# Triangular inversion of a chunked delta rule with its two 64-blocks laid over each other

## What is computed

```python
def gated_delta_chunked(q, k, v, g, beta, state0):
    ...
    decay = jnp.exp(jnp.where(incl, Gcum[..., :, None] - Gcum[..., None, :], -jnp.inf))
    kb = kc * bc[..., None]
    A = jnp.where(strict, jnp.einsum('bhnid,bhnjd->bhnij', kb, kc) * decay, 0.0)
    t_inv = lax.linalg.triangular_solve(A + eye, jnp.broadcast_to(eye, A.shape), left_side=True, lower=True, unit_diagonal=True)
    W = t_inv @ (kb * jnp.exp(Gcum)[..., None])
    U = t_inv @ (vc * bc[..., None])
    attn = jnp.einsum('bhnid,bhnjd->bhnij', qc, kc) * decay
    ...
    def step(S, xs):
        W_n, U_n, attn_n, qd_n, kt_n, gt_n = xs
        v_new = U_n - jnp.einsum('bhcd,bhde->bhce', W_n, S)
        o = jnp.einsum('bhcd,bhde->bhce', qd_n, S) + jnp.einsum('bhij,bhje->bhie', attn_n, v_new)
        S = S * gt_n[..., None, None] + jnp.einsum('bhcd,bhce->bhde', kt_n, v_new)
        return S, o
```

## Time and profile before

| | us |
|---|---|
| median of 3 runs | 1768.65 (1767.53 to 1769.34) |
| the profiled execution's own time | 1769.91 |
| its span on the core | 1768.1 |
| PE busy | 1712.0 |
| PE weight loads busy | 1535.7 |
| DVE busy | 1299.4 |
| ACT busy | 1075.2 |
| POOL busy | 161.9 |

### The profile page before, as it was taken

The page is one execution under the profiler, slowest core; times in us unless marked ns, Lnnn a source line. Parts: engine busy times, 40 slices in busy tenths (PEclk is TensorE's granted clock), DMA queues, the critical chain, the costliest instruction groups (busy, mean ns, idle before and its releaser), DMA issues.

```text
span 1768.1 us, 34099 instructions
## 1 busy us (share of the span) xinstructions
PE 1712.0 (97%) x11488; PEld 1535.7 (87%) x11488; DVE 1299.4 (73%) x2604; ACT 1075.2 (61%) x2222; POOL 161.9 (9%) x136
## 2 busy tenths in 40 slices
PE   7999998999999999999999999999899999999998
PEld 1877788989999977888899999999799899999997
DVE  3787667767989799667766666666776668878887
ACT  2545466645665699666555555555558666666666
POOL 0000004411638200000000000000010000010000
PEclk9899999999999999999999999999999999999999
DMA  8524441225455411555555555555354544555553
GB/s 301 185 99 143 153 158 62 82 71 190 158 178 188 157 37 38 180 193 196 190 190 184 185 189 185 184 189 190 119 205 143 172 137 134 178 184 185 189 181 129
DMA packets 77271, 283.30 MB, mean 160 GB/s; under 512 B 8576, under 2 KB 8576, under 8 KB 76928
## 3 DMA queue, kind: packets, MB, share of 16 engines
q1 hardware_dynamic: 77184, 282.16, 47.5%
HBM read 281.08 MB, written 1.05 MB: 160 GB/s over the span
## 4 chain that ended last, share of the span: by engine, by line
PE 80%; DVE 11%; ACT 5%; issue 1%; DMA 1%; POOL 1%; PEld 0%; PEldq 0%; SPq 0%; ACTq 0%; POOLq 0%; DVEq 0%
PE banks L901 20%; PE banks L889 17%; PE banks L980 9%; PE banks L491 8%; PE banks L1136 7%; PE banks L1160 3%; PE banks L831 2%; DVE split L2396 2%; DVE arena L2392 2%; PE banks L459 1%; DMA arena<-wstream 1%; PE banks L994 1%; PE banks L680 1%; PE banks L1096 1%; PE banks L665 1%
## 5 line engine op out<-in xcount | busy, mean ns | idle before, releaser
L1501 ACT ACTIVATE split<-arena 128x512 fp32r<-128x512 f32 x492 | 308.9, 629 | 135.0 <-PE banks L889 76.8
L889 PEld LDWEIGHTS banks<-split 128*128 128x128 f32 x2880 | 355.4, 192 | 10.5 <-DVE split L2322 3.1
L901 PE MATMUL banks<-split 128*128 128x512 f32 x1536 | 361.9, 390 | 1.0 <-issue 1.0
L889 PE MATMUL banks<-split 128*128 128x256 f32 x2880 | 358.7, 283 | 3.1 <-DVE split L2322 2.3
L2414 DVE TENSOR_TENSOR split<-arena,split 128x512 fp32r<-128x512 f32 x396 | 270.5, 690 | 105.3 <-ACT split L1501 99.5
L901 PEld LDWEIGHTS banks<-split 128*128 128x128 f32 x1536 | 283.8, 188 | 57.3 <-issue 1.4
L1479 ACT ACTIVATE split<-arena 128x512 fp32r<-128x512 f32 x312 | 194.5, 627 | 115.4 <-PE banks L1136 52.9
L980 PE MATMUL banks<-split 128*128 128x256 f32 x1728 | 218.1, 288 | 4.3 <-DVE split L2492 3.9
L980 PEld LDWEIGHTS banks<-split 128*128 128x128 f32 x1728 | 213.2, 195 | 7.2 <-issue 6.0
L2469 DVE TENSOR_TENSOR split<-arena,split 128x512 fp32r<-128x512 f32 x180 | 123.8, 698 | 67.5 <-ACT split L1479 66.0
L491 PEld LDWEIGHTS banks<-split 128*128 128x128 f32 (+1 forms) x936 | 134.3, 195 | 28.1 <-issue 14.1
(11 more groups left out here) (414 smaller groups left out, 2359.1 us busy)
## 6 DMA issues: line engine op xcount, KB each, us to landing
arena<-wstream SPq DMA_DIRECT2D x525, 512.0 KB, 3.3
arena<-x_t SPq DMA_DIRECT2D x1, 2048.0 KB, 13.0
arena<-matsa SPq DMA_DIRECT2D x1, 1234.0 KB, 6.5
out_t<-arena SPq DMA_DIRECT2D x4, 256.0 KB, 2.0
arena<-mats SPq DMA_DIRECT2D x1, 576.0 KB, 8.3
arena<-crow SPq DMA_DIRECT2D x1, 512.0 KB, 7.3
arena<-rows SPq DMA_DIRECT2D x1, 512.0 KB, 4.0
arena<-mats SPq DMA_DIRECT2D x1, 449.0 KB, 3.7
```

What stands on the lines that cost most here:

```text
L889: mm = pe.matmul(ps[:, 4 + b, 0:S], w_parts[:, c, (2 * m + half) % 4, P * k:P * k + P], h_parts[:, e, 4 * half + k, :], start=(half == 0 a ...
L901: mm = pe.matmul(ps[:, 2 * tt + half, :], g_parts[:, e, j % 2, P * tt:P * tt + P], w_parts[:, c, (2 * m + half) % 4, :], start=(first and ...
L1501: act.activation(w_parts[:, 0, (2 * m + half) % 4, :], ring[:, peer_slot(m), 512 * half:512 * half + 512], ACT.Copy).then_inc(sem["w_hi"], 1)
```

## The change

Up to level 5 nothing outside the two 64x64 diagonal blocks of each 128x128 matrix is used. The changed kernel lays these two over each other: partitions 0 to 63 hold the first block, partitions 64 to 127 the second, in the same 64 columns per head. The tiles `Z1`, `Z2` and the new `AO` (the keys laid over each other) have 4 x 64 = 256 columns instead of 512, a half of Z has 128, the packed keys have 128 per slot.

- Products: for each 64-block q one matmul with 64 rows (partitions 64q to 64q + 63), all four heads in it, into bank `2d + q`, and one transpose of 64 rows into the same bank behind it, columns 128 to 191. Order: transpose 0, transpose 1, product 0, product 1.
- One DVE eviction of both banks with a mask widened by ones (`masks`, built at the stage's start) takes products and transposes to `yp` (128 x 2 x 192). The tile `T`, ACT's copy to it and the semaphore `t_ready` are gone.
- Updates: for each q one matmul with all 128 rows and 64 output partitions, 64q to 64q + 63.
- The subtraction, `keep_half` and `pack_keys` work on 128 columns. `pack_keys` at level 1 first lays the keys over each other (two copies of 64 partitions, and a wait for them).
- Level 6 joins the two blocks: its products use the rows of one 64-block, its transposes those of the other, and its updates write the 64 partitions `rows_at(d)`. DVE evicts them in three copies for each direction, ahead of `first_inverse`, and writes the negated update to the new tile `Z` (128x512), the rest of which ACT fills from level 6's halves; the never-written quarter is set to zero at the stage's start.
- `first_inverse` takes four operations of 64 partitions x 128 columns for each direction instead of two of 128 x 256.
- `apply_inverse` writes the keys' part to bank `2d + 1`; the products of level 1 of the next step wait for `w_moved`, which ACT raises once `wt` is copied.

```diff
+        rows_at = lambda q: slice(64 * q, 64 * q + 64)
+        last_keys = lambda d: flat(pair[d]["AP"])[rows_at(1 - d), P:3 * P]
+        level_bank = lambda d, q: ps[:, 2 * d + q, :]
...
             def level_products(n, l, d):
...
                 pe.wait_ge(sem["keys_packed"], level_at(n, l, d))
-                for j in range(2):
-                    c = slice(P * j, P * j + P)
-                    mm = pe.matmul(ps[:, d, c], keys_at(d, l)[:, c], half_at(d, l, 1 - d)[:, c], start=True, stop=True)
-                mm.then_inc(sem["y_done"], 1)
                 if l == 1:
                     if n:
-                        pe.wait_ge(sem["wu_ready"], step_at(n - 1, d))
+                        pe.wait_ge(sem["w_moved"], step_at(n - 1, d))
                     else:
                         pe.wait_ge(sem["tok_ready"], 3 + d)
-                for j in range(2):
-                    mm = pe.transpose(ps[:, 2 + d, P * j:P * j + P], half_at(d, l, d)[:, P * j:P * j + P], ident)
-                mm.then_inc(sem["z_turned"], 1)
+
+                def product(q):
+                    c, r = slice(P * q, P * q + P), rows_at(q if l < 6 else 1 - d)
+                    keys, half = (keys_at(d, l)[r, :], half_at(d, l, 1 - d)[r, :]) if l < 6 else (last_keys(d)[:, c], inverse_at(d, 6)[r, c])
+                    return pe.matmul(level_bank(d, q)[:, 0:P] if l < 6 else level_bank(d, 0)[:, c], keys, half, start=True, stop=True)
+
+                def turn_half(q):
+                    c, r = slice(P * q, P * q + P), rows_at(q if l < 6 else d)
+                    half = half_at(d, l, d)[r, :] if l < 6 else inverse_at(d, 6)[r, c]
+                    return pe.transpose(level_bank(d, q)[:, P:P + 64] if l < 6 else level_bank(d, 1)[:, 64 * q:64 * q + 64], half, ident[r, r])
+
+                if l < 6:
+                    turn_half(0)
+                    turn_half(1).then_inc(sem["z_turned"], 1)
+                    product(0)
+                else:
+                    product(0)
+                    turn_half(0)
+                product(1).then_inc(sem["y_done"], 1)
+                if l == 6:
+                    turn_half(1).then_inc(sem["z_turned"], 1)
 
             def level_update(n, l, d):
                 pe.wait_ge(sem["y_out"], level_at(n, l, d))
-                pe.wait_ge(sem["t_ready"], level_at(n, l, d))
-                for j in range(2):
-                    mm = pe.matmul(ps[:, d, 256 + P * j:256 + P * j + P], pair[d]["T"][:, j, :], yp[d][:, j, :], start=True, stop=True)
+                for q in range(2):
+                    out = ps[rows_at(q), 2 * d, 256:384] if l < 6 else ps[rows_at(d), 2 * d, 256 + P * q:384 + P * q]
+                    mm = pe.matmul(out, yp[d][:, q, P:P + 64], yp[d][:, q, 0:P], start=True, stop=True)
                 mm.then_inc(sem["p_done"], 1)
...
             def pack_keys(n, l, d):
+                a, over = pair[d][f"A{n % 2}"], pair[d]["AO"].rearrange("p a (b s) -> p (a b) s", s=64)
                 if l == 1:
                     act.wait_ge(*((sem["mask_ready"], d + 1) if n == 0 else (sem["a_beta"], step_at(n - 1, d))))
-                act.activation(as_packed(keys_at(d, l), l), parts(flat(pair[d][f"A{n % 2}"]), l, d), ACT.Copy).then_inc(sem["keys_packed"], 1)
+                    for q in range(2):
+                        o = act.activation(over[rows_at(q)], a[rows_at(q), :, rows_at(q)], ACT.Copy)
+                    link(o)
+                if l < 6:
+                    o = act.activation(as_packed(keys_at(d, l), l), parts(flat(pair[d]["AO"]), l, d), ACT.Copy)
...
                     for d in range(2):
-                        if l == 6:
-                            act.wait_ge(sem["y_done"], level_at(n, l, d))
-                            for q in range(2):
-                                r = slice(64 * q, 64 * q + 64)
-                                o = act.activation(yp[d][r, :, r], bank(d, 2, P)[r, :, r], ACT.Copy)
-                            o.then_inc(sem["y_out"], 1)
-                        act.wait_ge(sem["z_turned"], level_at(n, l, d))
-                        act.activation(flat(pair[d]["T"]), ps[:, 2 + d, 0:256], ACT.Copy).then_inc(sem["t_ready"], 1)
...
+            for d in range(2):
+                dve.memset(pair[d]["Z"][rows_at(1 - d), :, rows_at(d)], 0.0)
+            dve.memset(masks[:, :, P:P + 64], 1.0)
+            link(dve.tensor_copy(masks[:, :, 0:P], blocks))
             tails = iter(range(EARLY_TAILS, 32))
...
                     for d in range(2):
+                        dve.wait_ge(sem["z_turned"], level_at(n, l, d))
+                        dve.wait_ge(sem["y_done"], level_at(n, l, d))
                         if l < 6:
-                            dve.wait_ge(sem["y_done"], level_at(n, l, d))
-                            dve.tensor_tensor(yp[d], bank(d, 2, P), bc(blocks[:, l - 1, :], 1, 2), ALU.mult).then_inc(sem["y_out"], 1)
-                        elif n < 3:
+                            o = dve.tensor_tensor(yp[d], ps[:, 2 * d:2 * d + 2, 0:P + 64], bc(masks[:, l - 1, :], 1, 2), ALU.mult)
+                        else:
+                            dve.tensor_copy(yp[d][:, :, P:P + 64], bank(2 * d + 1, 2, 64))
+                            for q in range(2):
+                                r = rows_at(q)
+                                o = dve.tensor_copy(yp[d][r, :, r], bank(2 * d, 2, P)[r, :, r])
+                        o.then_inc(sem["y_out"], 1)
+                    for d in range(2):
+                        if l == 6 and n < 3:
                             first_inverse(n + 1, d)
```

More of the change, by code:

```diff
@@ L238, in build @@
         at = buf("at", 4, 4, P)
-        PAIR = ("E", "A0", "A1", "Z0", "Z1", "Z2", "AP", "T", "KB", "VB", "KT", "S", "wt", "uu")
-        pair = [{n: buf(f"{n}{d}", 2 if n == "T" else 4, P) for n in PAIR} for d in range(2)]
-        yp = [buf(f"yp{d}", 2, P) for d in range(2)]
+        PAIR = ("E", "A0", "A1", "Z1", "Z2", "Z", "AO", "AP", "KB", "VB", "KT", "S", "wt", "uu")
+        TWO = ("Z1", "Z2", "AO")
+        pair = [{n: buf(f"{n}{d}", 2 if n in TWO else 3 if n == "AP" else 4, P) for n in PAIR} for d in range(2)]
+        yp = [buf(f"yp{d}", 2, P + 64) for d in range(2)]
+        masks = buf("masks", 5, P + 64)
         assert held["rstd"][0] == held["root"][0] + 512
@@ L655, in level_products @@
                 if l == 1:
-                    if n == 0 and d == 1:
+                    if n == 0 and d == 0:
                         pe.wait_ge(sem["proj_free"], 4 + 39)
@@ L694, in apply_inverse @@
                 for h in range(4):
-                    pe.matmul(ps[:, 2 + d, P * h:P * h + P], b["KB"][:, h, :], z[:, h, :], start=True, stop=True)
+                    pe.matmul(ps[:, 2 * d + 1, P * h:P * h + P], b["KB"][:, h, :], z[:, h, :], start=True, stop=True)
                 for h in range(4):
@@ L1422, in _ @@
                     act.wait_ge(sem["wu_done"], step_at(n, d))
-                    act.activation(pair[d]["wt"].rearrange("p a b -> p (a b)"), ps[:, 2 + d, :], ACT.Copy)
+                    act.activation(pair[d]["wt"].rearrange("p a b -> p (a b)"), ps[:, 2 * d + 1, :], ACT.Copy).then_inc(
+                        sem["w_moved"], 1)
                     act.activation(pair[d]["uu"].rearrange("p a b -> p (a b)"), ps[:, 6 + d, :], ACT.Copy).then_inc(sem["wu_ready"], 1)
@@ L2109, in first_inverse @@
                 dve.wait_ge(sem["m_turned"], step_at(n, d))
[L2110 to L2113 removed]
+                for r in (rows_at(0), rows_at(1)):
+                    for q in range(2):
+                        o = dve.tensor_tensor(half_at(d, 1, q)[r, :].rearrange("p (a b s) -> p a b s", a=4, s=2),
+                                              bc(ident[r, r].rearrange("p (b q s) -> p b q s", q=2, s=2)[:, :, q, :], 1, 4),
+                                              bank(4 + d, 4, P)[r, :, r].rearrange("p a (b q s) -> p a b q s", q=2, s=2)[:, :, :, q, :],
+                                              ALU.subtract)
                 o.then_inc(sem["z1_ready"], 1)
```

46 lines of the change are left out of this document (29 added, 17 removed).

## The result

The changed kernel is slower: 1781.78 us median of 5 runs (1772.43 to 1782.27) beside 1768.85 for the kernel before (1767.53 to 1769.83), ratio 1.0061, 95% interval 1.0039 to 1.0083. The forecast was 1764.3 with a range of 1758 to 1771. The profiled execution of after is the fastest of the five, 1772.43.

What follows compares the result with a forecast made beforehand. TensorE, busy nearly the whole span, was taken as the bound. Terms -5.0 - 1.35 - 0.5 - 1.3 + 2.95 + 0.85 = -4.35 us gave 1764.3 against the median of 1768.65, range 1758 to 1771.

Steps and rivals of the forecast that it cites:

- column groups pair: Updates on two column groups: the two matmuls pair as row groups do, taking two steps a direction; forecast 0.57.
- change of shape: Switching PE between 128-row and 64-row work costs 0.2 us a change, with two to four changes a level.
- groups A to D: Levels by kind: PE-bound -5.0, nothing between -1.35, level 1 of steps 1 to 3 -0.5, DVE-bound -1.3 us.
- B: Levels (0,5), (1,2), (2,2) with nothing between products and updates: 2.09 against 2.58 us in (1,2); together -1.35 us.
- unpaired columns: Rival: column groups don't pair, every update takes four steps; +5.3 us, so 1769.6; chance 0.22.
- free changes: Rival: changes of shape cost nothing or are hidden by loading weights ahead; -6.9 us more, 1757.4; chance 0.08.
- waiting weights: Rival: update records also wait for their weights, 0.21 each; +12.9 us, 1777.2; chance 0.08 for two slow cases together.
- products that do not pair: Rival: transposes and products keep 6 steps a direction; about +10 us, 1774; chance 0.08 for two slow cases together.
- Term E: Level 6: DVE does evictions and next first inverse before negated copies; +0.9, +0.9, +1.0, +0.15 by step, +2.95 us.
- Term F: Stage start: memsets, a copy, smaller inverses and more packs on DVE delay PE; +0.85 us over level (0,1).
- Applies and the end: Step applications, state products and all later stages: unchanged and following PE, so no term in the sum.
- granted clock still 1.00: Sign expected in the profile of after: granted clock stays at 1.00, as the table by stretch showed before.

## Why the prediction was wrong

**What held.** Row groups pair for products and transposes, column groups pair for updates, and the change of shape costs what the earlier trace rows said: the first update record starts 0.65 after 354.54, where five records of L724 take four steps of 0.111 and one of 0.20. The groups A to D were forecast at -8.15 and measured at -8.5. (The terms of B add up to 2.07, not 2.09; its levels measured 2.12.) The rivals on unpaired columns, free changes, waiting weights and products that do not pair are all out.

**Term E, level 6, was too small: +2.95 against +5.4.** The forecast let six evictions follow each other at 0.20 us and took 1.6 for eight half-size inverses. DVE in level 6 of step 1, in the trace of after:

```profile
312.97 0.29 DVE L2212 COPY arena<-banks 128x128 f32<-128x128 f32 x1 [0.22 <-PE banks L683]
...
313.18 0.58 DVE L2215 COPY arena<-banks 64x128 f32<-64x128 f32 x2
...
314.61 2.01 DVE L2140 TENSOR_TENSOR arena<-arena,banks 64x128 f32<-64x128 f32 x8
...
316.65 0.88 DVE L2227 TENSOR_SCALAR arena<-banks 64x256 f32<-64x256 f32 x2
```

The six evictions take 1.64 us, 0.27 each, and the inverses 2.04, 0.25 each: 3.68 us instead of 2.8. That is 0.88 of the 0.97 us by which the level is longer than forecast (4.97 against 4.0). The mis-sized step is "three small operations a direction, 0.20 apart, six in 1.2; first inverse in eight half-size ones, 1.6". How long one lasts was right: operations on PSUM with half the partitions last as long as those with all (282 against 289 ns, above). But in a row they start 0.25 to 0.27 apart on the mean, and the two copies L2215 of one direction 0.3. The Trainium skill, "Perfetto Trace Analysis", section Optimizing Scalar/DVE Operations, gives each DVE operation a fixed overhead, for PSUM about 125 ns, and says that larger operations can help where the engine is saturated. The trace agrees that splitting is paid for: eight half-size inverses last 2.01 us, four of 128 x 256 lasted 1.40. That both queues would wait in that order was foreseen, with the right waits; that it could be undone by moving three lines was not looked for.

**Term F, the start, was too small: +0.85 against +1.8.** The four operations in front of DVE's queue cost 0.7 on the path, by the run without them. The other 1.1 stands behind the three packs of ACT (1.18 us from 260.09 to 261.27, one pack before) and the eight inverses. The forecast named both, but its 0.85 is less than the 1.3 us that it gave the four operations alone, and it has no price for the packs.

**Applies and the end: 0 against +0.6.** They follow half-height work now, and each starts with a change of shape.

**The step that turned the sign: "granted clock still 1.00".** The forecast read 1.00 in the earlier trace rows and carried it over to a kernel that it said, in the same breath, would leave PE waiting for DVE in level 6. The nearest row of the stage, the single wait of 2.35 us in level 5 of step 1, bears it out, and that was not enough: the changed kernel has at least two more pauses in each of three steps and half-array work around them, and the trace of before has low clock behind such work and pauses elsewhere (1406.1, above). The cost should have been bounded from both sides like the other unknown prices: from nothing to a stretch of 3.4 us at 0.50 after each of four pauses, which costs at most half its length, 6.8 us in all by this estimate. The fastest profile has +6.0; the other two have +10.0 and +13.6. With terms E and F right the forecast would have been 1767.7, with all lengths as measured 1767.9, no change that can be told from noise; with the low clock of the profile at 1780.77 it is 1781.5. The experiments bear out that the pauses bring it: filling them with idle products gives back 10.6 us, putting pauses into the kernel before costs it 14, of which the path is 10, and removing the pauses of level 6 gives 13.8, of which the path is 5.7.

The Trainium skill, "TensorE: Matmul & The Clock Gate", section A second HAM failure mode: psum-queue depth-cycling, describes another kernel, in bf16, whose TensorE "micro-idles between MM groups frequently enough" that its clock swings between the two levels. The traces here agree in that short waits go with such swings (1.84 us in level 6 and 0.81 in front of its updates), though not each time. The prediction did not weigh it.

**What stays open.** Why the same kernel runs with 13.6 us of low clock in one execution and 34.2 in another, and whether removing 0.7 us at the start made the lighter case the common one, or whether that came with the other set of runs. Whether half-array work makes a pause count for more is not shown either. The runs show how long the clock was low, and what PE waited for in front of it, and no more.

## What to carry to other kernels

- Making PE's work shorter in a stage with waits makes the waits a larger share of it. Price each pause that a change opens on PE twice: once as path, and once as clock.
- When an engine takes over work that another did beside it, write its queue at that place in order of who waits: the result that PE needs goes first, the preparation of the next step behind it. Here that was worth 13.8 us, where the path of the change itself gained 0.75.
- If a pause can't be closed, some idle matmuls into a free bank are a cheap test of what it costs in clock, and may stay in.

## What the runs showed of the hardware

- Two column groups run at the same time for float32: two matmuls of four records each, 64 output rows, are eight records in 0.66 us. So do two row groups with transposes and products mixed: twelve records start within 0.82 us, where full-height ones took 1.60.
- A change between full-array work and either tiling costs about 0.2 us where PE was busy.
- DVE operations that read PSUM with 64 partitions x 128 elements take 282 to 290 ns, as those with 128 x 128 do.
- Pauses of 1.8 to 2.7 us on PE in the tiled stage had stretches of 3.4 to 6.9 us at 1.2 GHz in or behind them in most profiles, but not behind each pause. A single wait of 2.35 us between full-array work had none in two profiles. Each us at 1.2 GHz cost about 0.4 us here.
